# A depthwise convolution of 31 taps put wholly on TensorE, two output tokens at a time, beside block attention with its pairs of heads one slot deeper

## The reference

```
proj = rms_norm(x) @ w_in
attn = moba_attention(rope(rms_norm(q)), rope(rms_norm(k)), v)   # 256 tokens: one block, causal softmax
h    = (u_a + b_a) * sigmoid(u_g + b_g)                          # 512 channels
conv = sum over t of dw_w[t] * h[token - 30 + t] + dw_b          # 31 taps, one weight per channel and tap
conv = silu(layer_norm(conv) * ln_g + ln_b)
x    = x + concat(attn, conv) @ w_out
```

## Time and profile before

| what | value |
|---|---|
| median of 3 runs | 756.14 us (755.87 to 756.16) |
| profiled execution, its own time | 756.11 us |
| its span, first to last instruction | 754.3 us |
| PE busy | 749.9 us, 99% |
| PE weight loads busy | 620.8 us, 82% |
| DVE busy | 568.5 us, 75% |
| ACT busy | 400.9 us, 53% |
| chain that ended last | PE 95%, DVE 3%, ACT 1%, issue 1% |
| granted TensorE clock | 1.00 throughout |

### The profile page before, as it was taken

One profiled execution on the slowest core, in us unless ns is written; L12 is line 12 of the kernel. 1 busy time (PEld: TensorE's weight loads), 2 busy tenths in 40 slices (PEclk: granted clock), 3 DMA queues, 4 the chain that ended last, 5 costly groups with the idle time before them and its releaser, 6 DMA issues.

```text
span 754.3 us, 9798 instructions
## 1 busy us (share of the span) xinstructions
PE 749.9 (99%) x3820; PEld 620.8 (82%) x3820; DVE 568.5 (75%) x908; ACT 400.9 (53%) x524; POOL 50.8 (7%) x39
## 2 busy tenths in 40 slices
PE   9999999999999999999999999999999999999998
PEld 7888899888888888888888888887688888888887
DVE  6869789986767877687788748697658777768584
ACT  6765455646567546546555455655556344343430
POOL 0200000000002400000000000732000000000000
PEclk9999999999999999999999999999999999999999
DMA  9963434555363467565655575677034756565601
GB/s 313 386 221 95 157 120 161 195 169 162 117 219 116 167 212 261 182 219 175 218 179 178 200 222 206 227 188 271 2 113 147 244 179 211 171 210 177 222 3 56
DMA packets 71101, 137.12 MB, mean 182 GB/s; under 512 B 3216, under 2 KB 9232, under 8 KB 70928
## 3 DMA queue, kind: packets, MB, share of 16 engines
q1 hardware_dynamic: 70448, 136.37, 54.4%
q10 hardware_dynamic: 608, 0.14, 0.1%
HBM read 133.12 MB, written 1.05 MB: 178 GB/s over the span
## 4 chain that ended last, share of the span: by engine, by line
PE 95%; DVE 3%; ACT 1%; issue 1%; DVEq 0%; ACTq 0%
PE b L698 21%; PE b L700 21%; PE b L699 21%; PE SS L698 4%; PE SS L700 4%; PE SS L699 4%; PE TT L665 3%; PE OO L698 3%; PE OO L700 3%; PE OO L699 3%; DVE wlo L1668 1%; PE OO L1041 1%; PE b L871 1%; PE SS L817 1%; PE b L1041 1%; PE SS L835 1%
## 5 line engine op out<-in xcount | busy, mean ns | idle before, releaser
L1668 DVE TENSOR_TENSOR wlo<-raw,whi 128x2048 fp32r<-128x2048 f32 (+2 forms) x119 | 270.2, 2273 | 80.8 <-ACT whi L1205 80.1
L1205 ACT CAST whi<-raw 128x2048 fp32r<-128x2048 f32 (+2 forms) x119 | 222.9, 1878 | 124.3 <-PE b L700 85.9
L698 PE MATMUL b<-whi,Ahi 128*128 128x512 f32 (+2 forms) x520 | 204.0, 392 | 0.0
L700 PE MATMUL b<-whi,Alo 128*128 128x512 f32 (+2 forms) x520 | 199.5, 384 | 0.0
L699 PE MATMUL b<-wlo,Ahi 128*128 128x512 f32 (+2 forms) x520 | 199.3, 383 | 0.0
L700 PEld LDWEIGHTS b<-whi,Alo 128*128 128x128 f32 x520 | 97.9, 188 | 19.5
L698 PEld LDWEIGHTS b<-whi,Ahi 128*128 128x128 f32 x520 | 98.1, 189 | 18.6 <-ACT gates L1289 0.2
L699 PEld LDWEIGHTS b<-wlo,Ahi 128*128 128x128 f32 x520 | 98.1, 189 | 18.1
L2087 DVE STREAM_TRANSPOSE hT<-ust 32x256 f32<-32x256 f32 (+1 forms) x192 | 81.5, 425 | 2.7
L698 PE MATMUL b<-whi,Bhi 128*128 128x512 f32 x154 | 60.4, 392 | 0.1
L700 PE MATMUL b<-whi,Blo 128*128 128x512 f32 x154 | 60.0, 389 | 0.0
(11 more groups left out here) (311 smaller groups left out, 1023.2 us busy)
## 6 DMA issues: line engine op xcount, KB each, us to landing
raw<-in_w_in SPq DMA_DIRECT2D x38, 1024.0 KB, 5.1
raw<-in_w_up SPq DMA_DIRECT2D x16, 1024.0 KB, 5.4
raw<-in_w_dn SPq DMA_DIRECT2D x16, 1024.0 KB, 5.0
raw<-in_w_d SPq DMA_DIRECT2D x11, 1024.0 KB, 5.0
raw<-in_w_g SPq DMA_DIRECT2D x10, 1024.0 KB, 5.1
raw<-in_w_u SPq DMA_DIRECT2D x10, 1024.0 KB, 5.1
raw<-in_w_out SPq DMA_DIRECT2D x8, 1024.0 KB, 5.4
raw<-in_w_br SPq DMA_DIRECT2D x4, 1024.0 KB, 5.2
```

Of the source, the lines that this page charges most:

```text
L698: e.matmul(dst, xh, H[:, kc, c0:ce], start=(first or c0 == 768) and kc == krs[0], stop=False)
L700: ins = e.matmul(dst, xl, H[:, kc, c0:ce], start=False, stop=last and kc == krs[-1])
L1205: e.copy(whi[:, s, 0:m], raw[:, r, 0:m]).then_inc(s_hi, 1)
L1668: e.tensor_tensor(wlo[:, s, 0:m], raw[:, r, 0:m], whi[:, s, 0:m].bitcast(F32), ALU.subtract).then_inc(s_lo, 1)
```

## The change

1. A column strip of PE now holds 16 channels in two phases (even and odd tokens), and the rows hold eight shifts of 16 channels. A step covers 8 shifts for two output tokens, and its matmuls have 128 columns instead of 256. There are 32 steps instead of 28, and DVE has no taps left.
2. `ch` is stored by parity of the token. The 16 DMAs from SBUF to SBUF become 8 DMAs from `ch` into a buffer in the chip's memory (`shifts`) and 8 DMAs from there into `hs`, each into 16 partitions, 32 runs of 560 bytes for each partition. SP waits for the first eight (`d_ch`) ahead of the second eight. The load of the second `wo2` unit now stands between the two groups, and the third behind both.
3. `S2` has four slots instead of two; `at` and `ap` lag `az` by one and two pairs. The softmax's sum is no longer accumulated by ACT: `V2` has a 65th column of ones per head, and `aw` takes the reciprocal of the product's 65th column.
4. The convolution leaves PSUM by two DVE instructions of 512 columns instead of four of 256. The norm reads its rows as two halves of 256 elements per parity, and `ln_back` waits for both parities.

The core of the diff:

```diff
-        ch = sb("ch", [128, 4, 288], c=g2)
+        ch = sb("ch", [128, 4, 2, 144], c=g2)
...
-        S2 = sb("S2", [128, 3, 384], c=g2)
-        V2 = sb("V2", [128, 2, 512], c=g2)
+        S2 = sb("S2", [128, 4, 384], c=g2)
+        V2 = sb("V2", [128, 2, 8, 72], c=g2)
...
+    shifts = nc.dram_tensor("shifts", [16, 8, 1152], F32, kind="Internal").ap()
...
             if i == unit_of["wo2", 0, 1, 0]:
                 w.wait_ge(s_ug, 2)
-                for g in range(4):
-                    for s in range(4):
-                        e.dma_start(hs[32 * s:32 * s + 32, NTE * g:NTE * g + NTE, 0:284],
-                                    ch[32 * g:32 * g + 32, :, s:s + 284]).then_inc(d_hs, 16)
+                for q in range(8):
+                    e.dma_start(shifts[:, q, :], ch[16 * q:16 * q + 16].rearrange("p k r u -> p (k r u)")).then_inc(d_ch, 16)
+            if i == unit_of["wo2", 0, 1, 0] + 1:
+                w.wait_ge(d_ch, 128)
+                for s in range(8):
+                    src = shifts.rearrange("c q (k r u) -> c (q k) r u", k=4, r=2)
+                    e.dma_start(hs[16 * s:16 * s + 16, :, :, 0:140].rearrange("p q k u -> p (q k) u"),
+                                src[:, :, s % 2, s // 2:s // 2 + 140]).then_inc(d_hs, 16)
             load(i)
...
         def conv(m):
-            o, j = TAPS[m]
-            bk, c = TAPB[o % 2], 256 * (o // 2)
+            o, j = m // 4, m % 4
+            bk, c = TAPB[o // 4], 128 * (o % 4)
             if m == 0:
-                w.wait_ge(d_hs, 256)
+                w.wait_ge(d_hs, 128)
                 w.wait_ge(d_tw, 32)
...
             for g in range(4):
-                ins = e.matmul(bank[bk][32 * g:32 * g + 32, c:c + 256],
-                               tw[:, 32 * (4 * m + g):32 * (4 * m + g) + 32],
-                               hs[:, NTE * g + TILE[o], 4 * j:4 * j + 256], start=j == 0, stop=last)
+                ins = e.matmul(bank[bk][32 * g:32 * g + 32, c:c + 128], tw[:, 32 * (4 * m + g):32 * (4 * m + g) + 32],
+                               hs[:, 4 * (o % 2) + g, o // 2, 4 * j:4 * j + 128], start=j == 0, stop=j == 3)
...
         def am(h):
-            P = S2[:, h % 2, :]
-            nm, l = stat_m[h], stat_s[h]
+            P = S2[:, h % 4, :]
+            nm = stat_m[h]
             w.wait_ge(s_am, h + 1)
-            e.activation(P[:, 0:128], P[:, 0:128], ACT.Exp, bias=nm[:, 0:1], scale=-1.0, accum_out=l[:, 0:1])
+            e.activation(P[:, 0:128], P[:, 0:128], ACT.Exp, bias=nm[:, 0:1], scale=-1.0)
...
         def aw(p):
-            w.wait_ge(s_ae, 2 * p + 2)
-            k = own(e.reciprocal(l, l))
+            w.wait_ge(s_ap, p + 1)
             w.wait_ge(s_ut, 4)
-            w.wait_ge(s_ap, p + 1)
+            k = own(e.reciprocal(l, o[:, :, :, 64]))
             w.wait_ge(s_dve, k)
...
         def ln_back(p):
-            w.wait_ge(s_lv, p + 1)
+            w.wait_ge(s_lv, 2)
```

More of the change, by code:

```diff
@@ L31, in _layout @@
     for name, w in (("g_mlp", 8), ("g_fin", 8), ("g_n1", 8), ("g_n2", 8), ("glu_b", 8),
[L32 to L33 removed]
+                    ("room", 124), ("dw_b", 8), ("ln_g", 4), ("ln_b", 4), ("b_f", 4), ("lam", 128),
+                    ("g_diff", 64)):
         PAR[name] = (n, w)
@@ L462, in build @@
     rp8, rpv, rpr = [stat(8) for _ in range(4)], [stat(8) for _ in range(4)], [stat(8) for _ in range(4)]
-    bs, mv, lnv, lnr = [[stat(n) for _ in range(2)] for n in (6, 2, 1, 1)]
+    mv, lnv, lnr = [[stat(n) for _ in range(2)] for n in (2, 1, 1)]
+    bs = [lscr[:, 16 * i:16 * i + 12] for i in range(2)]
     r1c, r1cq = rpv[3][:, 0:4:2], rpv[3][:, 1:4:2]
@@ L1108, in tile_parts @@
                 n_conv[0] += 1
-        tile_parts(3)
-        for p in range(4):
-            az(p)
[L1113 to L1116, removed]
+        tile_parts(6)
+        az(0)
+        tile_parts(10)
+        az(1)
+        at(0)
+        for p in (2, 3):
+            tile_parts(4 if p == 2 else 3)
+            az(p)
+            ap(p - 2)
+            at(p - 1)
+        tile_parts(4)
+        ap(2)
+        at(3)
         tile_parts(2)
         ap(3)
-        tile_parts(1)
+        tile_parts(2)
         for t in range(2):
@@ L1131, in ln_turn @@
             clear(bk)
[L1132 to L1135, removed]
+            w.wait_ge(s_cf, p + 1)
+            turn4(bank[bk], cdv[:, 4 * p:4 * p + 4, :].rearrange("p o u -> p (o u)")).then_inc(s_l1, 1)
         def ln_back(p):
-            w.wait_ge(s_lv, p + 1)
+            w.wait_ge(s_lv, 2)
             turn4(bank[NBK[p]], ys[:, p, 512:1024]).then_inc(s_l2, 1)
@@ L1522, in evac2 @@
             else:
-                o = V2[:, t, :]
+                e.mul(V2[:, t, :, 0:64], bank[P2B[i % 2][t]].rearrange("p (h d) -> p h d", h=8), r).then_inc(s_ev, 1)
+                return
             e.mul(o, bank[P2B[i % 2][t]], r).then_inc(s_ev, 1)
@@ L2291, in _ @@
             am(2 * p + 1)
[L2292 to L2296, removed]
+            if p == 1:
+                taps_out(0)
+            if p > 1:
+                aw(p - 2)
+        aw(2)
         aw(3)
@@ L2299, in _ @@
         x_lo(("Y", 1, 0))
-        taps_out(3)
+        taps_out(1)
         def ln():
-            for p in range(2):
[L2304 to L2308, removed]
+            rows = [[bank[NBK[j]].rearrange("p (g r c) -> p r g c", r=2, c=16)[:, p] for j in range(2)] for p in range(2)]
+            for j in range(2):
+                w.wait_ge(s_l1, j + 1)
+                for p in range(2):
+                    k = own(e.bn_stats(bs[p][:, 6 * j:6 * j + 6], rows[p][j]))
+            for p in range(2):
+                w.wait_ge(s_dve, k if p == 1 else k - 1)
+                n = own(e.bn_aggr(mv[p], bs[p]))
+                w.wait_ge(s_dve, n)
                 variance(f"l{p}", lnv[p], mv[p][:, 1:2], 1)
@@ L2311, in ln @@
                 w.wait_ge(s_rs, RS[f"l{p}"] + 1)
-                e.tensor_scalar(ys[:, p, 512:1024], bank[NBK[p]], mv[p][:, 0:1], lnr[p], ALU.subtract,
-                                ALU.mult).then_inc(s_lv, 1)
+                for j in range(2):
+                    ins = e.tensor_scalar(ys[:, p, 512 + 256 * j:768 + 256 * j].rearrange("p (g c) -> p g c", c=16),
+                                          rows[p][j], mv[p][:, 0:1], lnr[p], ALU.subtract, ALU.mult)
+                ins.then_inc(s_lv, 1)
         w.wait_ge(s_pg, 4)
@@ L2501, in _shifts, with _phase_rows @@
     import numpy as np
[L2503 to L2507, removed]
-    return m.reshape(128, 128 * len(TAPS))
+    taps = dw.reshape(31, 8, 4, 16)
+    m = np.zeros((8, 16, 8, 4, 4, 2, 16), np.float32)
+    c = np.arange(16)
+    for s in range(8):
+        for j in range(4):
+            for p in range(2):
+                if 0 <= 8 * j + s - p <= 30:
+                    m[s, c, :, j, :, p, c] = taps[8 * j + s - p].transpose(2, 0, 1)
+    return m.reshape(128, 4096)
+def _phase_rows(v):
+    import numpy as np
+    return np.repeat(v.reshape(8, 4, 1, 16), 2, axis=2).reshape(8, 128).T
 def kernel(**inputs):
```

102 lines of the change are left out of this document (36 added, 66 removed).

## The result

The changed kernel takes 763.08 us (median of 4, 761.96 to 763.83) against 756.15: 1.0091 times, with a 95% interval from 1.0074 to 1.0108. It is slower by 6.9 us, and the interval lies clear of no change. The profiled execution is the slowest of the four, 763.83 us; its span is 762.0, 7.7 longer than before.

A forecast was written before the change was run, and what follows sets the result against it. PE's own work was taken to bound the attention stage. The terms -4.1 + 0.95 + 9.2 + 1.0 = +7.0 us, on 756.1, gave 763.1 us; eight-in-ten range 752.5 to 765.5, likeliest case 760.5 to 765.5.

The forecast's parts named there:

- The gain on PE: Attention stage: 128-column convolution records at 33 ns let Y's turns start 4.1 us earlier.
- The norm: Norm behind Y's turns: split statistics and outputs, and a first turn no longer hidden, lose 0.95 us.
- The detour: Shifted rows through memory: slow 16-partition reads delay the third wo2 unit's cast, so PE's first scores wait 9.2 us.
- The clock: PE after its idle stretches: a lower granted clock costs 1.0 us, from a range of 0 to 3.5.
- Width does not bind: Rival on the shifted-row reads: at 216 GB/s or better nothing is late; faster, 752.9 us, chance 0.28.
- Partial overlap: Rival on the shifted-row reads: 130 GB/s, reads 17.6 us, stall 5.2 us, time 758.1 us; chance 0.12.
- Records bound by issue: Rival on PE's convolution: 57.5 ns a record whatever its columns; 769 us with the stall, 758.7 without; chance 0.04.
- the lower bound: Shifted-row reads: if partitions do not matter and only the issue does, 8 x 0.67 = 5.4 us.

The follow-up runs named there:

- early version: The changed kernel with shifted-row reads 32 partitions wide, still eight writes, and the third wo2 unit loaded ahead of the reads; 752.97 us.
- the swap: The changed kernel with the load of the third wo2 unit ahead of the eight reads on SP's queue instead of behind them; 761.26 us.
- wide version: The changed kernel with four reads of 32 partitions instead of eight of 16, and 16 writes of half the size instead of eight; 758.45 us.

## Why the prediction was right

The time came out as forecast (763.1 against 763.08), for the reason given, but the exact hit is luck: three terms were off, by -0.6, -0.9 and +1.8 us, and nearly cancelled. They are read from the profiled execution, which was 0.7 us over the median. By its own steps:

- **The gain on PE, 4.1.** In the early version Y's turns start at 538.78 instead of 543.55, which is 4.8; its steps begin 0.1 earlier, so 4.7. Started one behind the other, 48 records take 1.45 us there (520.77 to 522.22), 30.2 ns each, so the line through the earlier trace rows with its 30.8 was better than my 33, and a record did not cost the same whatever its columns.
- **The norm, 0.95.** PE went on 7.61 us later than before in the changed kernel (562.52 against 554.91 in the earlier trace rows), of which 6.49 were there at Y's turns: 1.1. Leaving the split out gave back 1.0 in the median and 1.1 in the trace. Ahead of the four outputs DVE now waits 0.36 us for POOL's root of the variance, a wait that the sum did not have.
- **The detour, 9.2.** The first scores start at 530.55 against 522.22 in the early version: 8.3. The chain of events was as laid out, each within 1.1 us: shifted rows at 524.6 (forecast 525.1), cast at 527.05 (528.1), last copy's end 530.5 (531.6). Within it two errors offset each other. The reads ran at 108 to 124 GB/s where I had taken 106 (half of 216 is 108), and from 502 to 522 the windows already add up to 2.4 MB, more than the reads' 2.29. Yet PE's wait for the rows ended only at 524.60; why is open. That width slows the reads is shown by the 32- and 128-partition runs, and the part of the queue's order by the swap.
- **The clock, 1.0.** Mis-sized: it cost 2.7 to 2.9. From the first scores to Y's turns the changed kernel took 19.49 us and the early version 16.56. I had the bound (0 to 3.5) and no row to choose by, and went too low. The bound itself was not well reckoned: two scores and ten steps are 4.4 us, 3.5 holds one score only. With 3.5 the time would be 765.6, not the 764.6 that stands there. The two idle stretches are 4.2 and 5.0 us by the prediction's own times of day, not 4.3 and 4.6.
- **Which rival.** "Width does not bind" is out: at 16 partitions the rate was 108 to 124 in the changed kernel. "Partial overlap", priced at 130 GB/s, is out for its traced execution but not for these reads in general: with the third unit ahead the same reads ran at 140 to 152, about the 147 at which the prediction has the stall eat the gain. "Records bound by issue" is out.

What I had not seen: I doubted that the 0.67 us of an issue was a limit, and still used it for the lower bound. In the changed kernel a write took 0.42 us to issue, and a read 0.62 to 4.3 us. The long ones came once several reads had been issued and not yet landed, so an issue's length in a trace need not be the price of issuing.

The Trainium skill, page "SBUF — State Buffer", section "Door 1: The DMA port swizzle", puts partitions 0 to 15 at about 109 GB/s at most. The changed kernel's trace roughly agrees (108 to 124). Two other traces do not: the same reads with the third unit ahead ran at 140 to 152, and runs of 9216 bytes at 148. In all of them several reads to different sets of 16 partitions stood in the queue; whether neighbours overlapped was not measured.

## What to carry to other kernels

When data is laid out anew by DMA, count the partitions that one transfer reaches before its bytes: 16 at a time took two to three times as long as 128 here. A small transfer in an ordered queue costs what stands behind it, so look first at which load is next, and at what is queued on the engine that casts it. If a stall of some microseconds on TensorE is weighed, add the time at the lower clock behind it, which was a third of the stall here.

## What the hardware showed that I had not expected

- One wait can be enough for the lower clock, and its length alone does not tell. In the version with the third unit ahead, PE was idle for 3.55 us, and the granted clock was 0.57 from 524 to 528; in the wide version a single wait of 3.36 us ahead of the first scores was followed by 0.50 from 528 to 532. The changed kernel's first wait was 3.36 us too, and behind it the clock was 1.00 (525 to 526); it fell to 0.50 only at the end of the second.
- The rate does not fall in proportion to the width: 328 and 333, 186 to 206, and 103 to 152 GB/s for 128, 32 and 16 partitions with short runs. In proportion from 328 it would be 82 and 41 for the last two.
- The same narrow reads ran at 103 to 124 GB/s in two traces and at 140 to 152 in another. With the third unit ahead of them the time went from 758.01 to 763.07 us on one chip, where the versions without a stall stay within 0.3 to 1.8 us. Why the rate differs is open; only the fastest of these executions was traced.
